# Experts' gate and up projections with the weights stationary and the tokens moving

## What is computed

```python
def _swiglu(h, w_gate, w_up, w_down):
    return (jax.nn.silu(h @ w_gate) * (h @ w_up)) @ w_down

def _moe_swiglu(h, router, w_gate, w_up, w_down):
    ...
    def expert_block(args):
        x_blk, e = args
        return _swiglu(x_blk, w_gate[e], w_up[e], w_down[e])

    yb = lax.map(expert_block, (xb, block_e)).reshape(-1, d)
    y = jnp.zeros_like(xt).at[s_tok].add(yb[dest] * s_gate[:, None].astype(xt.dtype))
    return y.reshape(shp)
```

## Time and profile before

| | us |
|---|---|
| median of 3 runs | 3394.6 (3394.48 to 3395.17) |
| the profiled execution | 3390.67 |
| its span, first to last instruction | 3388.9 |
| TensorE busy in the span | 3127.3 (92%) |
| TensorE's granted clock, mean | 0.96 |
| one item, gather to gather | 155.82 |
| bytes moved by the DMA engines | 560.51 MB |

### The profile page before, as it was taken

One profiled execution on the slowest core, in us unless ns is written; L12 is line 12 of the kernel. 1 busy time (PEld: TensorE's weight loads), 2 busy tenths in 40 slices (PEclk: granted clock), 3 DMA queues, 4 the chain that ended last, 5 costly groups with the idle time before them and its releaser, 6 DMA issues. The chain is left out here.

```text
span 3388.9 us, 36490 instructions
## 1 busy us (share of the span) xinstructions
PE 3127.3 (92%) x15033; PEld 1793.8 (53%) x15033; DVE 972.1 (29%) x1979; ACT 465.6 (14%) x957; POOL 174.7 (5%) x210
## 2 busy tenths in 40 slices
PE   8889899799887899999799886999999999999998
PEld 6558788644476344444344675444444444444444
DVE  1446476437644233100146543000000000000001
ACT  1300000123422100000132321100000000001000
POOL 0000000000142000000000330000000000000000
PEclk9999999899998899999899997999999999999999
DMA  7145566321300243222122100988898888888885
GB/s 237 63 166 182 186 236 219 105 91 50 77 3 2 75 149 112 75 74 74 54 98 80 24 3 9 323 285 284 268 298 271 293 273 296 271 298 270 296 272 173
DMA packets 291964, 560.51 MB, mean 165 GB/s; under 512 B 28241, under 2 KB 40909, under 8 KB 291835
## 3 DMA queue, kind: packets, MB, share of 16 engines
q1 hardware_dynamic: 270755, 497.71, 44.6%
q0 software_dynamic: 13856, 53.11, 4.4%
q10 hardware_dynamic: 7223, 7.85, 0.8%
HBM read 557.42 MB, written 1.23 MB: 165 GB/s over the span
## 5 line engine op out<-in xcount | busy, mean ns | idle before, releaser
L1150 PE MATMUL bank<-normed,weight_ring 128*128 128x256 f32 (+1 forms) x2240 | 676.4, 464 | 35.7 <-PEq L1221 23.4
L1150 PEld LDWEIGHTS bank<-normed,weight_ring 128*128 128x128 f32 x2240 | 432.8, 194 | 271.9 <-issue 233.4
L2454 PE MATMUL bank<-weight_ring,work 128*128 128x512 f32 x1024 | 449.5, 593 | 10.1 <-ACT work L2487 10.1
L2454 PE MATMUL bank<-work 128*128 128x512 f32 x768 | 337.5, 592 | 0.0
L2454 PEld LDWEIGHTS bank<-weight_ring,work 128*128 128x128 f32 x1024 | 192.2, 190 | 241.0 <-issue 241.0
L656 PE MATMUL bank<-normed,weight_ring 128*128 128x512 f32 (+1 forms) x704 | 283.5, 564 | 24.7 <-PEq L1221 24.7
L1150 PE MATMUL bank<-work,weight_ring 128*128 128x256 f32 (+1 forms) x896 | 282.4, 475 | 9.2 <-PEq L1126 9.2
L2508 DVE TENSOR_TENSOR work<-bank,work 128x512 f32<-128x512 f32 x56 | 38.7, 692 | 788.5 <-PE bank L2454 788.5
L217 DVE SCALAR_TENSOR_TENSOR work<-work,small 128x512 f32<-128x512 f32 x336 | 237.6, 749 | 13.0 <-DMA work<-in_mod_w 6.1
L2454 PEld LDWEIGHTS bank<-work 128*128 128x128 f32 x768 | 144.8, 190 | 175.9 <-issue 175.9
L1150 PEld LDWEIGHTS bank<-work,weight_ring 128*128 128x128 f32 x896 | 172.0, 192 | 115.9 <-issue 102.3
(11 more groups left out here) (332 smaller groups left out, 2576.8 us busy)
## 6 DMA issues: line engine op xcount, KB each, us to landing
weight_ring<-in_moe_w_gate SPq DMA_DIRECT2D x64, 1024.0 KB, 5.1
weight_ring<-in_moe_w_up SPq DMA_DIRECT2D x64, 1024.0 KB, 5.1
weight_ring<-in_moe_w_down SPq DMA_DIRECT2D x64, 1024.0 KB, 5.0
work<-in_mod_w POOLq DMA_DIRECT2D x48, 1024.0 KB, 6.4
work<-in_moe_w_gate SPq DMA_DIRECT2D x48, 1024.0 KB, 5.1
work<-in_moe_w_up SPq DMA_DIRECT2D x48, 1024.0 KB, 5.1
work<-in_moe_w_down SPq DMA_DIRECT2D x48, 1024.0 KB, 5.0
weight_ring<-in_w_in SPq DMA_DIRECT2D x36, 1024.0 KB, 5.3
```

Source lines behind the costliest of these rows:

```text
L1150: last = nc.tensor.matmul(banks(gi)[j][:, 0:a.shape[-1]], w[:, k, j * P:(j + 1) * P], a, start=k0 + k == 0, stop=k0 + k == total - 1)
L2454: last = nc.tensor.matmul(self.bank[b], xg[:, kk], w[:, k], start=kk == 0, stop=kk == DT - 1)
```

## The change

Gate and up exchange the roles of the operands. For each bank both of its tiles are waited for (`pair`), and then each of four blocks `c` of 128 features is computed by 8 matmuls into 128 columns of the bank: the block of the weights is stationary, `xg[:, kk]` is moving, 128 columns. The bank then has features on partitions and tokens along its columns, and VectorE's product is what the down projection needs. It goes straight to `hid`. `turn_hidden`, `move_hidden` and their semaphores are gone; the down projection waits on `mult` instead, for six products before it starts and for the seventh ahead of its last tile in the first bank. The wait that the scatter's banks are free (`added`), which `turn_hidden` had, stands ahead of the scatter.

```diff
-                    def turn_hidden(q):
-
-                        pe.wait_ge(mult.sem, x * n_col + mult.at(q + 1))
-                        if q >= 2:
-                            pe.wait_ge(moved.sem, x * n_col + moved.at(q - 1))
-                        else:
-                            pe.wait_ge(added.sem, x * 2 + added.at(2))
-                        for c in range(4):
-                            last = nc.tensor.transpose(self.bank[4 + q % 2][:, c * P:(c + 1) * P], hk[:, q % 2, c * P:(c + 1) * P], ident)
-                        last.then_inc(turned.sem, 1)
-
...
                         for b in (2 * (q % 2), 2 * (q % 2) + 1):
-                            for i in range(n_in):
-                                w = next_tile()
-                                for k in range(TILE_K):
-                                    kk = i * TILE_K + k
-                                    last = nc.tensor.matmul(self.bank[b], xg[:, kk], w[:, k], start=kk == 0, stop=kk == DT - 1)
-                                last.then_inc(used.sem, 1)
-                        if q >= 1:
-                            turn_hidden(q - 1)
+                            pair = [next_tile() for _ in range(n_in)]
+                            for c in range(4):
+                                for kk in range(DT):
+                                    last = nc.tensor.matmul(self.bank[b][:, c * P:(c + 1) * P], pair[kk // TILE_K][:, kk % TILE_K, c * P:(c + 1) * P], xg[:, kk],
+                                                            start=kk == 0, stop=kk == DT - 1)
+                                    if c == 3 and kk % TILE_K == TILE_K - 1:
+                                        last.then_inc(used.sem, 1)
+                    pe.wait_ge(mult.sem, x * n_col + mult.at(n_col - 1))
                     for b in range(2):
                         for i in range(n_down):
                             w = next_tile()
-                            if b == 0:
-                                pe.wait_ge(moved.sem, x * n_col + moved.at(i + 1))
+                            if b == 0 and i == n_down - 1:
+                                pe.wait_ge(mult.sem, x * n_col + mult.at(n_col))
...
                             last.then_inc(used.sem, 1)
-                            if b == 0 and i == 0:
-                                turn_hidden(n_col - 1)
+                    pe.wait_ge(added.sem, x * 2 + added.at(2))
                     for b in range(2):
...
-                    def move_hidden(q):
-                        act.wait_ge(turned.sem, x * n_col + turned.at(q + 1))
-                        nc.scalar.activation(hid[:, 4 * q:4 * q + 4].rearrange("p k s -> p (k s)"), self.bank[4 + q % 2], ACT.Copy).then_inc(moved.sem, 1)
-
...
-                        if q >= 1:
-                            move_hidden(q - 1)
-                    move_hidden(n_col - 1)
...
-                        nc.vector.tensor_tensor(hk[:, q % 2], self.bank[2 * (q % 2) + 1], hk[:, q % 2], ALU.mult).then_inc(mult.sem, 1)
+                        h = hid[:, 4 * q:4 * q + 4].rearrange("p k s -> p (k s)")
+                        nc.vector.tensor_tensor(h, self.bank[2 * (q % 2) + 1], hk[:, q % 2], ALU.mult).then_inc(mult.sem, 1)
```

## The result

The changed kernel takes 3443.8 us (median of 4 runs, 3442.4 to 3445.2) against 3394.9 of the kernel before. The ratio is 1.0143, with a 95% interval of 1.013 to 1.0155. It is slower, as forecast, but by 48.9 us and not by 16.2, and outside the range of 3396.6 to 3430. Its profiled span is 3443.4 us, 54.5 over the old one, of which 3.4 lie ahead of the first item's gather, where nothing was changed. (The execution profiled before was 4.2 us under that median, this one is 1.5 over its own.)

A forecast was written before the change was run, and what follows sets the result against it. It took TensorE's row as the bound in the experts, with memory close behind. Gate and up +5.7 us and code refetching +10.5 us made +16.2 us, 3394.6 to 3410.8 us; range 3396.6 to 3430.

The forecast's parts named there:

- The pace: In gate and up, each new half of 128 moving columns lasts 111.5 ns from start to start.
- the rival that the moving columns would set the pace: Gate and up halves at 109.3 ns: -10 us if code is kept, no change with refetches; 4% in all.
- the rival that weight traffic slows the loads: Gate and up halves at 117 ns instead of 111.5: 39 us more, about 3450 or 3440; 8%.
- The net of +0.7 us an item: New gate and up, 99.9 us, against old with transposes, 99.2; +5.7 us for 8 items.
- The edits at nothing: ScalarE's dropped copies, VectorE's product into `hid` and the new waits cost nothing, as TensorE's work covers them.
- The code: TensorE's longer loop body is likelier refetched than kept at the branch back; 10.5 us on 7 branches, 65%.
- the price of a branch: At the loop's end, a 3.5 us fetch less the sequencer's 2.0 us lead leaves 1.5 us a branch.
- the far end of the bounds: For the code fetch at the branch, a landing of 6.5 us, leaving 4.5 us a branch.
- The clock: At the gather: a 1.5 us stop does not cost the clock, a longer one could; nothing counted.
- The upper end of the range: Refetch with a 5.1 us landing (21.7 us) and the 112.1 ns pace (10 us): 3426; 3430 leaves room.
- The lead: At the loop's end the sequencer is 2.0 us ahead of the array after branching; a shorter fetch is free.
- The length: TensorE's new loop body has 2,112 instructions, 8.5 to 9 packets; by the skill's 2048 it does not fit.

The follow-up runs named there:

- a_hint: The changed kernel plus one hint at the top of TensorE's loop body, naming the branch at its end so its target can be fetched early; 3402.4 us.
- a_rot: The changed kernel with TensorE's loop turned, so that the branch stands amid the down projection, same matmuls in the same order; 3401.7 us.
- a_quiet: The changed kernel with the last weight load ahead of an item's boundary held back by one more tile use, some 17 us; 3411.2 us.
- b_inc8: The kernel before with 8 unused semaphore increments behind each matmul of gate, up and down, 1,344 instructions more an item; 3942.2 us.

## Why the prediction was wrong

**The pace was right.** I took 111.5 ns a half, from the gather's rows and L1470's; the new halves run at 111.6 (the earlier trace rows and the rows after). L231's single moving column pointed to the weight load as the limit, which no run tested by changing the load; the rival that the moving columns would set the pace (109.3) did not come, nor the rival that weight traffic slows the loads. The net of +0.7 us an item came out as +0.93 in a_hint and a_rot: 0.8 by the measured pace, and 0.1 because TensorE's wait for the gathered tokens is 1.37 us instead of 1.26. This term was sized 5.7 us and measured at 7.4.

**The edits at nothing cost nothing.** No half waits for a weight tile, and the waits on `mult` and `added` do not show. ScalarE's saved copies bring nothing. (One reading was loose: the last of the fifteen DMA digits of the earlier trace rows is 5, not 8 or 9; nothing rests on it.)

**The code: the mechanism was right, its price was not.** "I take refetching as likelier than keeping" held, packets and all. The step that failed is the price of a branch, "nearest to 16 KB is the router's 32 KB load, 3.5 us": the branch takes 6.2 us. What it had wrong is what stands ahead of the packet: the branch comes 0.8 us behind a weight load of 1 MB, and 2.7 of the 6.2 us go behind it; with that load out of the way a_quiet's branch takes 3.5 us. That this is the router's number too is luck. The router's load was not a quiet one either (a load of 512 KB was issued 0.4 us ahead of it, and in the three microseconds from 2081 the DMA engines' share was 0.82 to 1.07), and its 3.5 us are a landing, where a_quiet's are the sum 1.1 + 1.0 + 1.3. I named the crowded landing of 6.5 us as the far end of the bounds instead of asking which loads stand ahead at this moment. The earlier trace rows and the slots' order were enough to see it: SyncE issues a tile whenever one is used, and the last of them is used just before the scatter. So the stall is 3.75 us in the mean and not 1.5: 26.3 us instead of 10.5.

**The clock was left out, the second term that failed.** I wrote that "a longer one could" cost it and gave the price of an idle time of 4.05 us, a gather of 5.92 us instead of 3.73, and then counted nothing for it, because my stall was 1.5 us. It is 16.2 us, a third of the loss. The two errors hang together: a wait that is longer by 2.3 us was dearer by 2.3 + 2.3. The upper end of the range, made of a stall of 3.1 us without the clock, was too low for the same reason.

**The lead was about right**: I had 2.0 us between a finished branch and the next load, and 6.2 us of branch left 3.75 of idle time, a lead of 2.4 with the branch's own time in it. Ten packets came in an item where I expected 8 to 9.

**The length.** The Trainium skill (Runtime: NRT & Kernel Launch, Instruction fetch mechanics) says 2048 instructions for TensorE, in blocks of 256, and a stall for a taken branch whose target is not in the current 2-page window. The stall is there, and packets of 16 KB. Neither length holds for this loop: 1,781 instructions were already not kept, and 1,598 were, more than six blocks. Here the measurement decides. Whether the limit is at seven blocks, or depends on how the body lies across blocks, was not tried.

## What to carry to other kernels

Count a hardware loop's instructions on each engine when an edit makes its matmuls smaller: past a length, each trip pays for fetching the code, at the branch, and the profile shows it as idle time ended by "issue", as a long COMPARE_BRANCH on the sequencer and as packets in the instruction queue. If the body cannot be shortened, hint the branch, or put it where the engine's queue holds more work than the fetch takes, here amid the long matmuls of the down projection and not behind the short scatter. When a wait is priced from a similar one elsewhere, take the one with the same loads ahead of it in the DMA queues, and ask at once whether the array's idle time is long enough to cost the clock.

## What the runs showed of the hardware

- TensorE kept a loop body of 1,598 instructions and did not keep one of 1,781. Past the limit nine packets are fetched in each trip for 1,781 instructions, which fill 7.0, and not only the excess.
- A branch to code that is not there takes 3.4 to 3.8 us with quiet DMA engines and 5.8 to 6.5 when a 1 MB load was issued 0.8 us ahead of it; one to code that is there 0.22 us; a hinted one 0.36 us, although nine packets of its loop's code are fetched in each trip.
- In the changed kernel idle times of 3.35 to 3.99 us were followed by a gather at partly 1.2 GHz at all seven boundaries; in b_inc8 those of 2.85 to 3.23 us at six of seven (not one of 2.90); those of 2.0 us and less at none. Sixteen matmul halves of spare work in the gap saved 13 us.
- With f32 weights, halves of 128 moving columns follow each other at 111.6 ns, as those of one column do (111.4), so the moving columns do not set the pace; that the load of the weights does was not tested. Against 429 ns for 512 columns that is 4% more for the same sum.
- A semaphore increment between matmuls is not hidden by them: eight of them behind each matmul of 858 ns lengthened an item from 155.8 to 225.2 us. Each lasts 51 ns in the trace, but they follow each other 0.15 us apart.
